# Forgetting-attention scores: two 64-row products per pair of heads and a separate product for the key decay, with two sets of probability buffers

## Chip, cores and metric

The kernel runs on one core of one Trainium2 chip. The metric is device time in microseconds (us) of one execution. All inputs, among them 227.94 MB of transfers by the profile, are read from device memory within that time.

## What is computed

The reference is a model of two blocks, each of two layers, over 512 tokens of 1024 features, in float32. The change touches one part of the first block's layers, the forgetting attention of six heads of 64 features:

```python
def fox_attention(q, k, v, log_f):
    c = jnp.cumsum(log_f, axis=1)                 # 512 tokens x 6 heads
    ...
        logits = jnp.einsum('bqhd,bkhd->bhqk', qb, k).astype(jnp.float32) * scale
        logits = logits + jnp.transpose(cb, (0, 2, 1))[..., None] - c_k
        causal = kpos[None, :] <= qpos[:, None]
        logits = jnp.where(causal, logits, NEG)
        w = jax.nn.softmax(logits, axis=-1)
        return jnp.einsum('bhqk,bkhd->bqhd', w.astype(v.dtype), v)
```

So every score of query q and key k gets c[q] - c[k] added, where c is the running sum of the log forget gates. A number added to a whole row of scores (c[q]) drops out of the softmax.

## The kernel before

Features lie on the partitions and tokens along the free axis. Large products are made from float32 values split into a high and a low part of type fp32r: `pe_tile` (L399) issues three matmuls of 512 columns (L404, L405, L406) for each tile of 128 features. Weights come as units of 128x1024: a transfer, a copy on ACT (L413, `w_hi`), a subtraction on POOL (L500, `w_lo`), then 24 matmuls.

Each layer of the first block runs, in this order on PE (`a_tensor`, L1187): the projection, the index scores (L1253), the forgetting attention ("fox", L1267), stick-breaking attention (L847 to L880), sparse attention ("dsa", L1282), and dense stages. Between the steps of the attention stages PE works off shares of 24 further units, the gate projection (`gate_share`); these are the rows L404 to L406 that stand between the attention's own.

Fox takes 12 pairs of heads and query blocks per layer: three pairs of heads, each with four blocks of 128 queries, so that the scores of a pair are 128, 256, 384 and 512 keys wide in turn. `pairs_pe`, `pairs_act` and `pairs_dve` write out the order by hand, each on its engine:

- PE, step n: scores of pair n+1 (L592, one product per head, then the mask L595), a share of gate tiles, the turning of pair n's probabilities (L605), another share, the products of pair n-1 with the values (L619). Where `ready` names a semaphore for the scores of pair n+1 (n+1 = 4 and 8), they stand behind the turning instead.
- DVE: row maxima of pair n+1 (L685), reciprocal and scaling of its probabilities (L693, L700), then one round of the index top-k search (L1560, L1562) and what `fox_after` adds. After pair 0 that is also the index-score work L1652, L1654.
- ACT: gate tiles that are due (L1363, L413), the exponentials of pair n+1 (L657), the copy of pair n's turned probabilities (L666).

The products of head e read `work[e]` and `work[2+e]`, 128 rows each: rows 0 to 63 are queries or keys, staged there by ACT (`fox_stage`, L1428), rows 64 to 127 are written by DVE (L1624, L1630) and carry c and selecting ones. With these four tiles taken, the probabilities have one set of buffers (`depth=1`): ACT's exponentials of pair n+1 wait until PE has turned pair n, and its copy of pair n waits for the value products of pair n-1.

In the sparse attention, heads 0 and 1 of a pair stand in rows 0 to 63 and 64 to 127 of the projection's tiles and are read there (`tile_rows`), as products of 64 rows.

Of the kernel before, what the change touches and what calls it, by code (L numbers as in the profile page):

```python
# [24 lines left out]
P = 128  # L25
# [52 lines left out]
C_ID, C_ROT, C_TRI, C_CAUS, C_STRICT, C_ST01, C_CHUNK = (P * n for n in range(7))  # L78
C_QA = 7 * P
C_QB = C_QA + 6  # L80
C_KA = C_QB + 6
C_KB = C_KA + 1
C_N = C_KB + 1

# [34 lines left out]
def plan(nc, ctx):  # L119
# [5 lines left out]
    def at(name, shape, dt, kb):  # L125
# [43 lines left out]
               for e, places in enumerate(((WK + 11.5, WK + 13.5, WK + 15, WK + 16), (128, WK + 16.5, 174, 175)))]  # L169
    S.c = at("log_f_sum", [P, SEQ], F32, WK + 16)  # L170
    o = [(WK + 18) * 1024]

# [73 lines left out]
    S.mask_ready = sem("mask_ready")  # L246
    S.fox_staged = sem("fox_staged")
    S.fox_aug = sem("fox_aug")
    S.stk_z = sem("stk_z")
# [304 lines left out]
class Pair:  # L554

    def __init__(self, S, n, b, key, mask, value, bank, heads=(0, 1), gate=None, first=None, begins=True, ends=True, depth=2):
        self.b, self.w = b, (b + 1) * P
        self.key = key
        self.mask = mask
        self.value = value  # L560
        self.bank = bank
        self.heads = heads
        self.gate = gate
        self.first = first
        self.begins, self.ends = begins, ends
        x = n % depth
        self.probs, self.turned = ((S.wk[4:6], S.wk[6:8]), (S.wk[0:2], S.wk[2:4]))[x]
        self.par = n % 2
# [11 lines left out]
def pairs_pe(S, pe, Z, h0, p0, pairs, ident, fill, ready, depth=2, lead=None):  # L580
# [3 lines left out]
    def scores(n):  # L584

        h = pairs[n]
        pe.wait_ge(Z.p, h0 + count_before(pairs, n))
        for sem, count in ready(n, "scores"):
            pe.wait_ge(sem, count)
        for e in h.heads:  # L590
            q, k = h.key(e)
            nc.tensor.matmul(S.X[e][:, 0:h.w], q, k, start=True, stop=False, skip_group_check=True)  # L592
        m, c = h.mask
        for e in h.heads:
            nc.tensor.matmul(S.X[e][:, c:h.w], S.idb[:, :], m, start=False, stop=True, skip_group_check=True).then_inc(Z.s, 1)  # L595
# [115 lines left out]
def fox_pairs(S):  # L711

    pairs = []
    for n in range(3 * QB):
        i, b = divmod(n, QB)
        w = (b + 1) * P
        pairs.append(Pair(S, n, b, lambda e, b=b, w=w: (S.wk[e][:, b * P:w], S.wk[2 + e][:, 0:w]), (S.causb[:, :], b * P),
                          lambda e, k, i=i: vt_head(S, k, V_FOX, 2 * i + e), (S.ps[3], S.X[3])[i % 2], depth=1))
    return pairs
# [467 lines left out]
def a_tensor(S, pe):  # L1187
    nc = S.nc
    ident = S.con[:, C_ID:C_ID + P]
    for L in range(DEPTH):  # L1190
# [68 lines left out]
        def fox_ready(n, what):  # L1259
            i = n // QB  # L1260
            if what == "scores" and n % QB == 0:
                return [(S.fox_staged, (L * 3 + i + 1) * 4), (S.fox_aug, (L * 3 + i + 1) * 2)]
            if what == "values" and n == 2 * QB:
# [92 lines left out]
def a_scalar(S, act, T):  # L1356
# [12 lines left out]
    for L in range(DEPTH):  # L1369
# [54 lines left out]

        def fox_stage(e, i):
            src = S.qkv[64 * e:64 * e + 64, :]
            for t, u in ((e, A_FQ), (2 + e, A_FK)):
                nc.scalar.activation(S.wk[t][0:64, :], cols2(src, u * SEQ, i, SEQ, SEQ), ACT.Copy).then_inc(S.fox_staged, 1)  # L1428

        act.wait_ge(S.rope_done, (L + 1) * len(ROPE))  # L1430
        for n, (b, h) in enumerate(idx_steps()):
            if n in (12, 16):
                fox_stage(n // 4 - 3, 0)
            act.wait_ge(S.idx_ready, L * 24 + n + 1)
# [14 lines left out]

        def fox_after(n):  # L1450
            if n % QB == 2 and n < 2 * QB:
                for e in range(2):
                    fox_stage(e, n // QB + 1)

        pairs_act(S, act, S.fox, L * 24, L * 12, fox_pairs(S), fox_after, depth=1,
                  before=lambda n: round_gates(FOX_FILL, n))
# [137 lines left out]
def a_vector(S, dve):  # L1594
    nc = S.nc
    for L in range(DEPTH):
# [24 lines left out]
        dve.drain()  # L1621
        nc.vector.tensor_copy(f, na)
        for e in range(2):
            nc.vector.tensor_scalar(S.wk[2 + e][64:128, :], na, S.con[64:128, C_KA:C_KA + 1], S.con[64:128, C_KB:C_KB + 1],  # L1624
                                    ALU.mult, ALU.add)

        def fox_rows(e, i):

            qa, qb = cols2(S.con[64:128, :], C_QA + e, i, 2, 1), cols2(S.con[64:128, :], C_QB + e, i, 2, 1)
            nc.vector.tensor_scalar(S.wk[e][64:128, :], f, qa, qb, ALU.mult, ALU.add).then_inc(S.fox_aug, 1)  # L1630

        dve.drain()
        for e in range(2):
            fox_rows(e, 0)

# [3 lines left out]
        for n, (b, h) in enumerate(idx_steps()):  # L1639
# [6 lines left out]
            else:  # L1646
                nc.vector.scalar_tensor_tensor(out=acc, in0=S.r[n % 2][:, 0:w], scalar=iw, in1=acc, op0=ALU.mult,
                                               op1=ALU.add).then_inc(S.idx_acc, 1)
            dve.drain()
        def index_scores():  # L1650
            for b in range(1, QB):
# [10 lines left out]
        def fox_after(n):  # L1662
            if n % QB == 2 and n < 2 * QB:
                for e in range(2):
                    fox_rows(e, n // QB + 1)
            if n == 0:
# [1050 lines left out]
def constants():  # L2717
# [11 lines left out]
    for h in range(6):  # L2729
        c[96 + h, C_QA + h] = 1.0  # L2730
        c[64 + h, C_QB + h] = 1.0
    c[64:96, C_KA] = -1.0
    c[96:, C_KB] = 1.0
    return c
# [40 lines left out]
```

## Time and profile before

| | |
|---|---|
| median of 3 executions | 2654.56 us (2651.69 to 2655.14) |
| the profiled execution | span 2653.1 us; no time of its own beside the span is given |
| PE busy | 2565.0 us, 97% |
| DVE, ACT, POOL busy | 59%, 43%, 40% |
| granted TensorE clock, mean over the span | 0.99 |

PE is TensorE's matmuls, DVE VectorE, ACT ScalarE, POOL GpSimd. A product of two float32 operands shows in the trace as two matmuls, so a pair of heads has four rows under L592. A matmul's length counts from its start to its end, and the next starts before that end; what a matmul costs is therefore read from one start to the next.

### The profile page before, as it was taken

How to read it: one execution, taken by the hardware profiler on the slowest of the kernel's cores; microseconds unless marked ns; L12 is line 12 of the kernel's file. 1: busy time of each engine (PE TensorE's matmuls, PEld its weight loads, DVE VectorE, ACT ScalarE, POOL GpSimd, SP SyncE). 2: the span in 40 equal slices, each digit the busy share in tenths (PEclk: the TensorE clock that was granted, in tenths of full speed). 3: DMA queues.
4: the chain of work that ended last, by engine and by line, in shares of the span. 5: the costliest groups of instructions: out<-in, count | busy, mean ns of one | idle time of the engine just before them, and what ended most of it. 6: DMA issues, size and time to landing. Idle time of an engine off the chain costs nothing.

```text
span 2653.1 us, 35398 instructions
## 1 busy us (share of the span) xinstructions
PE 2565.0 (97%) x12424; PEld 1983.9 (75%) x12424; DVE 1565.4 (59%) x2510; ACT 1147.6 (43%) x1984; POOL 1062.1 (40%) x440
## 2 busy tenths in 40 slices
PE   8999999999999899999999999998999999999998
PEld 6867667788888688676677888885887776887776
DVE  6147748843322751676588234227689766689765
ACT  3345444433322433544535233325247554347554
POOL 4432213354444344222233454442447512447512
PEclk9999999999999999999999999998999999999999
DMA  5321112233233243111122223231334211234211
GB/s 201 100 80 56 48 48 87 72 103 97 93 96 102 71 124 100 64 61 49 48 96 88 95 95 98 93 109 49 95 96 147 80 33 53 91 101 148 75 38 56
DMA packets 66891, 227.94 MB, mean 86 GB/s; under 512 B 8784, under 2 KB 8912, under 8 KB 66768
## 3 DMA queue, kind: packets, MB, share of 16 engines
q1 hardware_dynamic: 66192, 224.73, 26.2%
q8 instruction: 76, 1.25, 0.2%
q10 hardware_dynamic: 576, 1.57, 0.2%
q14 instruction: 47, 0.39, 0.0%
HBM read 216.57 MB, written 2.10 MB: 82 GB/s over the span
## 4 chain that ended last, share of the span: by engine, by line
PE 74%; DVE 12%; DVEq 9%; ACT 2%; issue 2%; POOL 0%; ACTq 0%; DMA 0%; SPq 0%
PE bank L404 20%; PE bank L406 19%; PE bank L405 19%; DVEq L2337 5%; PE bank L592 3%; PE bank L619 3%; PE bank L605 2%; PE bank L595 1%; PE bank L873 1%; DVEq L2359 1%; PE bank L1253 1%; PE bank L847 1%; DVE ffn_sum L1796 1%; PE bank L1225 1%; PE bank L1224 1%
## 5 line engine op out<-in xcount | busy, mean ns | idle before, releaser
L500 POOL TENSOR_TENSOR w_lo<-w_raw,w_hi 128x1024 fp32r<-128x1024 f32 x404 | 1017.8, 2527 | 1575.6 <-ACT w_hi L413 1569.7
L404 PE MATMUL bank<-x_hi,w_hi 128*128 128x512 f32 x2048 | 828.8, 405 | 28.3 <-DVE x_lo L2567 10.6
L406 PE MATMUL bank<-x_hi,w_lo 128*128 128x512 f32 x2048 | 804.9, 393 | 0.0
L405 PE MATMUL bank<-x_lo,w_hi 128*128 128x512 f32 x2048 | 803.5, 392 | 0.0
L413 ACT ACTIVATE w_hi<-w_raw 128x1024 fp32r<-128x1024 f32 x400 | 419.5, 1055 | 439.7 <-PE bank L406 355.3
L404 PEld LDWEIGHTS bank<-x_hi,w_hi 128*128 128x128 f32 x2048 | 388.4, 190 | 128.4 <-issue 29.7
L406 PEld LDWEIGHTS bank<-x_hi,w_lo 128*128 128x128 f32 x2048 | 387.8, 189 | 83.6
L405 PEld LDWEIGHTS bank<-x_lo,w_hi 128*128 128x128 f32 x2048 | 388.6, 190 | 75.0 <-issue 1.2
L404 PE MATMUL bank<-rhs_hi,w_hi 128*128 128x512 f32 x624 | 245.2, 393 | 3.3 <-DVE rhs_lo L1698 3.3
L405 PE MATMUL bank<-rhs_lo,w_hi 128*128 128x512 f32 x624 | 243.7, 390 | 0.0
L406 PE MATMUL bank<-rhs_hi,w_lo 128*128 128x512 f32 x624 | 243.4, 390 | 0.0
L1780 DVE TENSOR_TENSOR ffn_sum<-ffn_sum,bank 128x512 f32 x64 | 43.9, 688 | 286.3 <-PE bank L406 286.3
L657 ACT ACTIVATE work<-bank,neg_max 128x128 f32<-128x128 f32 (+3 forms) x216 | 112.0, 523 | 182.4 <-DVE neg_max L685 146.0
L1770 DVE TENSOR_TENSOR work<-work 128x512 f32<-128x512 f32 x64 | 93.9, 1467 | 135.1 <-ACT rhs_hi L1518 135.1
L2334 DVE SCALAR_TENSOR_TENSOR bank<-glu_out,params_b_cur,bank 128x512 f32<-128x512 f32 x216 | 152.7, 753 | 34.8 <-issue 34.8
L404 PEld LDWEIGHTS bank<-rhs_hi,w_hi 128*128 128x128 f32 x624 | 117.6, 188 | 33.5 <-issue 8.6
L406 PEld LDWEIGHTS bank<-rhs_hi,w_lo 128*128 128x128 f32 x624 | 117.6, 188 | 24.4
L405 PEld LDWEIGHTS bank<-rhs_lo,w_hi 128*128 128x128 f32 x624 | 117.5, 188 | 23.8
L685 DVE TENSOR_REDUCE neg_max<-bank 128x1 f32<-128x128 f32 (+3 forms) x216 | 96.1, 485 | 56.8 <-PE bank L595 55.1
L1516 ACT ACTIVATE work<-bank 128x512 f32<-128x512 f32 x64 | 37.9, 592 | 191.8 <-PE bank L406 183.9
L666 ACT ACTIVATE work<-bank 128x128 f32<-128x128 f32 (+3 forms) x216 | 83.1, 436 | 50.5 <-PE bank L619 31.6
L1772 DVE TENSOR_TENSOR rhs_lo<-work,rhs_hi 128x512 f32 x64 | 86.6, 1354 | 12.1 <-issue 12.1
(410 smaller groups left out, 3248.0 us busy)
## 6 DMA issues: line engine op xcount, KB each, us to landing
w_raw<-w SPq DMA_DIRECT2D x404, 512.0 KB, 3.4
work<-proj SPq DMA_DIRECT2D x60, 64.0 KB, 2.0
ln_in<-x SPq DMA_DIRECT2D x4, 512.0 KB, 7.2
out<-residual SPq DMA_DIRECT2D x8, 256.0 KB, 2.1
p_raw<-p ACTq DMA_DIRECT2D x2, 512.0 KB, 3.5
silu_z_nsa<-b_q SPq DMA_DIRECT2D x16, 64.0 KB, 2.3
work<-b_q SPq DMA_DIRECT2D x16, 64.0 KB, 2.3
silu_z_nsa<-b_kc SPq DMA_DIRECT2D x8, 64.0 KB, 2.0
```

The costliest lines, as they stand in the source:

```text
L404: nc.tensor.matmul(out, wh, xh, start=first, stop=False)
L405: nc.tensor.matmul(out, wh, xl, start=False, stop=False)
L406: S.last = nc.tensor.matmul(out, wl, xh, start=False, stop=last)
L413: S.nc.scalar.activation(S.wh[s][:, :], S.raw[s][:, :], ACT.Copy).then_inc(S.hi_ready[s], 1)
L500: S.nc.gpsimd.tensor_tensor(S.wl[s][:, :], S.raw[s][:, :], S.wh[s][:, :].bitcast(F32), ALU.subtract).then_inc(S.lo_ready[s], 1)
L657: nc.scalar.activation(h.probs[e][:, 0:h.w], S.X[e][:, 0:h.w], ACT.Exp, bias=S.nm[x][:, :], accum_out=S.rs2[:, x:x + 1]).then_inc(Z.p, 1)
L666: nc.scalar.activation(h.turned[e][:, 0:h.w], (S.X[2], S.ps[2])[e][:, 0:h.w], ACT.Copy).then_inc(Z.ptc, 1)
L685: nc.vector.tensor_reduce(S.nm[2 * h.par + e][:, :], S.X[e][:, 0:h.w], AX, ALU.max, negate=True).then_inc(Z.max, 1)
L1770: nc.vector.tensor_tensor(h, S.wk[j % 2][:, :], S.wk[j % 2][:, :], ALU.mult)
L1772: nc.vector.tensor_tensor(cols(S.rl, i * SLOTS + j), h, cols(S.rh, i * SLOTS + j).bitcast(F32), ALU.subtract).then_inc(S.ffn_h, 1)
L2334: stt(out=S.X[t % 2][:, :], in0=S.uc[:, bass.ds(i * 3 + (k + t * UC_W), SEQ)], scalar=S.curB[:, bass.ds(i * 3 + (k + PB_DW + t * CONV_K), ...
L2337: dve.drain()
```

## The change

The scores' product takes 64 rows per head straight from the projection's tiles. The key decay becomes a product of its own (`decay`): `cpick`, 64 rows by 128 columns of minus one in the two rows of the head, times `cparts`, in which row h holds the high part of c of head h and row 32+h the rest, both repeated in rows 64 to 127, in fp32r. The query's c is left out, as it drops out of the softmax. The staging copies on ACT and the augmented rows on DVE go; DVE fills `cparts` once a layer before the index scores and `cpick` right after them, where its place in memory comes free. Fox's pairs use two sets of probability buffers (`depth` 2).

```diff
--- before.py
+++ after.py
@@ -76,11 +76,8 @@
 
 
 C_ID, C_ROT, C_TRI, C_CAUS, C_STRICT, C_ST01, C_CHUNK = (P * n for n in range(7))
-C_QA = 7 * P
-C_QB = C_QA + 6
-C_KA = C_QB + 6
-C_KB = C_KA + 1
-C_N = C_KB + 1
+C_PART = 7 * P
+C_N = C_PART + 3
 
 
 PA_G1, PA_B1, PA_G2, PA_B2, PA_BF, PA_N = 0, 8, 16, 24, 32, 33
@@ -168,6 +165,8 @@
     S.stk_w = [[at(f"stick_weights{e}_{i}", [P, SEQ - i * P], F32, kb) for i, kb in enumerate(places)]
                for e, places in enumerate(((WK + 11.5, WK + 13.5, WK + 15, WK + 16), (128, WK + 16.5, 174, 175)))]
     S.c = at("log_f_sum", [P, SEQ], F32, WK + 16)
+    S.cparts = at("log_f_parts", [P, SEQ], F32R, WK + 16)
+    S.cpick = at("log_f_pick", [P, 3 * P], F32R, 128)
     o = [(WK + 18) * 1024]
 
     def small(name, n, dt=F32):
@@ -244,8 +243,7 @@
     S.relu_done = sem("relu_done")
     S.idx_acc = sem("idx_acc")
     S.mask_ready = sem("mask_ready")
-    S.fox_staged = sem("fox_staged")
-    S.fox_aug = sem("fox_aug")
+    S.fox_decay = sem("fox_decay")
     S.stk_z = sem("stk_z")
     S.stk_na = sem("stk_na")
     S.stk_ln = sem("stk_ln")
@@ -553,9 +551,10 @@
 
 class Pair:
 
-    def __init__(self, S, n, b, key, mask, value, bank, heads=(0, 1), gate=None, first=None, begins=True, ends=True, depth=2):
+    def __init__(self, S, n, b, key, mask, value, bank, heads=(0, 1), gate=None, first=None, begins=True, ends=True, depth=2, decay=None):
         self.b, self.w = b, (b + 1) * P
         self.key = key
+        self.decay = decay
         self.mask = mask
         self.value = value
         self.bank = bank
@@ -590,6 +589,9 @@
         for e in h.heads:
             q, k = h.key(e)
             nc.tensor.matmul(S.X[e][:, 0:h.w], q, k, start=True, stop=False, skip_group_check=True)
+        for e in h.heads if h.decay else ():
+            pick, parts = h.decay(e)
+            nc.tensor.matmul(S.X[e][:, 0:h.w], pick, parts, start=False, stop=False, skip_group_check=True)
         m, c = h.mask
         for e in h.heads:
             nc.tensor.matmul(S.X[e][:, c:h.w], S.idb[:, :], m, start=False, stop=True, skip_group_check=True).then_inc(Z.s, 1)
@@ -714,8 +716,9 @@
     for n in range(3 * QB):
         i, b = divmod(n, QB)
         w = (b + 1) * P
-        pairs.append(Pair(S, n, b, lambda e, b=b, w=w: (S.wk[e][:, b * P:w], S.wk[2 + e][:, 0:w]), (S.causb[:, :], b * P),
-                          lambda e, k, i=i: vt_head(S, k, V_FOX, 2 * i + e), (S.ps[3], S.X[3])[i % 2], depth=1))
+        pairs.append(Pair(S, n + 1, b, lambda e, b=b, w=w, i=i: (tile_rows(S, A_FQ + i, e)[:, b * P:w], tile_rows(S, A_FK + i, e)[:, 0:w]),
+                          (S.causb[:, :], b * P), lambda e, k, i=i: vt_head(S, k, V_FOX, 2 * i + e), (S.ps[3], S.X[3])[i % 2],
+                          decay=lambda e, w=w, i=i: (S.cpick[half(e), i * P:(i + 1) * P], S.cparts[half(e), 0:w])))
     return pairs
 
 
@@ -1257,9 +1260,8 @@
 
         pe.wait_ge(S.relu_done, (L + 1) * 24)
         def fox_ready(n, what):
-            i = n // QB
-            if what == "scores" and n % QB == 0:
-                return [(S.fox_staged, (L * 3 + i + 1) * 4), (S.fox_aug, (L * 3 + i + 1) * 2)]
+            if what == "scores" and n == 0:
+                return [(S.fox_decay, (L + 1) * 2)]
             if what == "values" and n == 2 * QB:
                 return [(S.fox.out, L * 3 + 1)]
             return []
@@ -1422,15 +1424,8 @@
                 if end == c:
                     gate_take(fill[0] + j)
 
-        def fox_stage(e, i):
-            src = S.qkv[64 * e:64 * e + 64, :]
-            for t, u in ((e, A_FQ), (2 + e, A_FK)):
-                nc.scalar.activation(S.wk[t][0:64, :], cols2(src, u * SEQ, i, SEQ, SEQ), ACT.Copy).then_inc(S.fox_staged, 1)
-
         act.wait_ge(S.rope_done, (L + 1) * len(ROPE))
         for n, (b, h) in enumerate(idx_steps()):
-            if n in (12, 16):
-                fox_stage(n // 4 - 3, 0)
             act.wait_ge(S.idx_ready, L * 24 + n + 1)
             if n >= 2:
                 act.wait_ge(S.idx_acc, L * 24 + n - 1)
@@ -1447,12 +1442,7 @@
             for x in range(2):
                 gate_takes(fill[i], calls[i], 2 * m + x)
 
-        def fox_after(n):
-            if n % QB == 2 and n < 2 * QB:
-                for e in range(2):
-                    fox_stage(e, n // QB + 1)
-
-        pairs_act(S, act, S.fox, L * 24, L * 12, fox_pairs(S), fox_after, depth=1,
+        pairs_act(S, act, S.fox, L * 24, L * 12, fox_pairs(S), lambda n: None,
                   before=lambda n: round_gates(FOX_FILL, n))
         round_gates(FOX_FILL, 3 * QB)
         nc.scalar.preload_act_table_set("natural_log_exp_and_others")
@@ -1619,19 +1609,12 @@
         dve.drain()
         nc.vector.tensor_tensor_scan(na, S.wk[4][64:128, :], f, 0.0, ALU.mult, ALU.add)
         dve.drain()
-        nc.vector.tensor_copy(f, na)
-        for e in range(2):
-            nc.vector.tensor_scalar(S.wk[2 + e][64:128, :], na, S.con[64:128, C_KA:C_KA + 1], S.con[64:128, C_KB:C_KB + 1],
-                                    ALU.mult, ALU.add)
-
-        def fox_rows(e, i):
-
-            qa, qb = cols2(S.con[64:128, :], C_QA + e, i, 2, 1), cols2(S.con[64:128, :], C_QB + e, i, 2, 1)
-            nc.vector.tensor_scalar(S.wk[e][64:128, :], f, qa, qb, ALU.mult, ALU.add).then_inc(S.fox_aug, 1)
-
+        nc.vector.tensor_copy(S.cparts[64:128, :], na)
         dve.drain()
-        for e in range(2):
-            fox_rows(e, 0)
+        rest = S.cparts[96:128, :]
+        nc.vector.tensor_tensor(rest, S.wk[5][96:128, :], rest.bitcast(F32), ALU.subtract)
+        dve.drain()
+        nc.vector.tensor_copy(S.cparts[0:64, :], S.cparts[64:128, :].bitcast(F32)).then_inc(S.fox_decay, 1)
 
         dve.wait_ge(S.bank_free[A_SPARE % SLOTS], G(A_SPARE) + 1)
         free_bank(S, dve, A_SPARE)
@@ -1647,6 +1630,10 @@
                 nc.vector.scalar_tensor_tensor(out=acc, in0=S.r[n % 2][:, 0:w], scalar=iw, in1=acc, op0=ALU.mult,
                                                op1=ALU.add).then_inc(S.idx_acc, 1)
             dve.drain()
+        for i in range(3):
+            m = nc.vector.tensor_copy(S.cpick[:, i * P:(i + 1) * P], S.con[:, C_PART + i:C_PART + i + 1].to_broadcast([P, P]))
+        m.then_inc(S.fox_decay, 1)
+
         def index_scores():
             for b in range(1, QB):
                 nc.vector.memset(S.sacc[0:64, SC0[b] + b * P + 64:SC0[b] + (b + 1) * P], NEG)
@@ -1660,9 +1647,6 @@
             nc.vector.tensor_copy(otok(S, tile)[rows, :], bank[rows, :]).then_inc(Z.out, 1)
 
         def fox_after(n):
-            if n % QB == 2 and n < 2 * QB:
-                for e in range(2):
-                    fox_rows(e, n // QB + 1)
             if n == 0:
                 index_scores()
             for x in range(2):
@@ -2727,10 +2711,8 @@
     c[:, C_ST01:C_ST01 + P] = i < j
     c[:, C_CHUNK:C_CHUNK + P] = np.where(j // 64 > i // 64, NEG, 0.0)
     for h in range(6):
-        c[96 + h, C_QA + h] = 1.0
-        c[64 + h, C_QB + h] = 1.0
-    c[64:96, C_KA] = -1.0
-    c[96:, C_KB] = 1.0
+        for part in range(2):
+            c[64 * (h % 2) + 32 * part + h, C_PART + h // 2] = -1.0
     return c
 
 
```

The order of the programs shows three places. First PE at the start of fox in the first layer, before the change; `work_96/97` are the keys, `work_94/95` the queries, `x_hi,w_hi` rows are gate tiles:

```order
L404 MATMUL bank<-x_hi,w_hi_54 128x512
L405 MATMUL bank<-x_lo,w_hi_54 128x512
L406 MATMUL bank<-x_hi,w_lo_58 128x512
L592 MATMUL bank<-work_96,work_94 128x128
L592 MATMUL bank<-work_97,work_95 128x128
L595 MATMUL bank<-causal_bf,ident_bf 128x128 x2
L404 MATMUL bank<-x_hi,w_hi_55 128x512
L405 MATMUL bank<-x_lo,w_hi_55 128x512
L406 MATMUL bank<-x_hi,w_lo_59 128x512
```

The same place after the change (the line numbers are those of the changed kernel):

```order
L402 MATMUL bank<-x_hi,w_hi_54 128x512
L403 MATMUL bank<-x_lo,w_hi_54 128x512
L404 MATMUL bank<-x_hi,w_lo_58 128x512
L591 MATMUL bank<-proj 128x128 x2
L594 MATMUL bank<-log_f_parts,log_f_pick 128x128 x2
L597 MATMUL bank<-causal_bf,ident_bf 128x128 x2
L402 MATMUL bank<-x_hi,w_hi_55 128x512
L403 MATMUL bank<-x_lo,w_hi_55 128x512
L404 MATMUL bank<-x_hi,w_lo_59 128x512
```

The two 128-row products became two 64-row products of `proj`, followed by the two decay products; the mask and the gate tiles behind it stand as before.

Second, PE around the first scores of the second pair of heads. Before the change, step 3 with its turning (x4 for each head) and the scores of pair 4 behind it:

```order
L406 MATMUL bank<-x_hi,w_lo_57 128x512
L605 MATMUL bank<-constants,work_98 128x128 x4
L605 MATMUL bank<-constants,work_99 128x128 x4
L592 MATMUL bank<-work_96,work_94 128x128
L592 MATMUL bank<-work_97,work_95 128x128
L595 MATMUL bank<-causal_bf,ident_bf 128x128 x2
L404 MATMUL bank<-x_hi,w_hi_53 128x512
```

After it, the scores of pair 4 behind the value products of pair 1 and ahead of the gate tiles:

```order
L621 MATMUL bank<-work_100,v_tok 64x128
L621 MATMUL bank<-work_101,v_tok 64x128
L591 MATMUL bank<-proj 128x128 x2
L594 MATMUL bank<-log_f_parts,log_f_pick 128x128 x2
L597 MATMUL bank<-causal_bf,ident_bf 128x128 x2
L402 MATMUL bank<-x_hi,w_hi_53 128x512
L403 MATMUL bank<-x_lo,w_hi_53 128x512
```

They moved forward past one share of gate tiles and the turning, to the place that they have in every other step.

Third, DVE at the end of the index scores, before:

```order
L1647 SCALAR_TENSOR_TENSOR idx_sum<-idx_relu_72,v_tok,idx_sum 128x512
L1647 SCALAR_TENSOR_TENSOR idx_sum<-idx_relu_73,v_tok,idx_sum 128x512
L685 TENSOR_REDUCE neg_max_115<-bank 128x1
L685 TENSOR_REDUCE neg_max_116<-bank 128x1
L693 RECIPROCAL gate_inv<-row_sums 128x2
```

and after the change, with the pick tiles between the last index sum and the first row maximum:

```order
L1630 SCALAR_TENSOR_TENSOR idx_sum<-idx_relu_72,v_tok,idx_sum 128x512
L1630 SCALAR_TENSOR_TENSOR idx_sum<-idx_relu_73,v_tok,idx_sum 128x512
L1634 CAST log_f_pick<-constants 128x128 x3
L687 TENSOR_REDUCE neg_max_119<-bank 128x1
L687 TENSOR_REDUCE neg_max_120<-bank 128x1
L695 RECIPROCAL gate_inv<-row_sums 128x2
```

PE's first scores wait for that last `log_f_pick` row (`fox_decay`), where they waited for ACT's and DVE's staging, long done, before.

## Rows read from the trace of the kernel before

**Rows 1.** The page, busy time of each engine over the span.
```profile
PE 2565.0 (97%) x12424; PEld 1983.9 (75%) x12424; DVE 1565.4 (59%) x2510; ACT 1147.6 (43%) x1984; POOL 1062.1 (40%) x440
```

**Rows 2.** Windows, fox, first layer: length, busy PE, PEld, DVE, ACT, POOL, clock, DMA.
```profile
187.00:270.50 83.50, 81.63 (x453) 60.45 (x452) 65.56 (x179) 38.97 (x96) 21.55 (x9) 1.00 0.16 51
```

**Rows 3.** Timeline of PE in fox: start, length, engine, line, what.
```profile
211.22 1.03 PE L605 MATMUL bank<-constants,work 128*128 128x128 f32 x8
212.36 0.68 PE L592 MATMUL bank<-work,work 128*128 128x128 f32 x4
212.88 0.28 PE L595 MATMUL bank<-causal_bf,ident_bf 128*128 128x128 bf16 x2
...
229.25 1.98 PE L592 MATMUL bank<-work,work 128*128 128x512 f32 x4
231.07 0.28 PE L595 MATMUL bank<-causal_bf,ident_bf 128*128 128x128 bf16 x2
...
266.65 1.04 PE L605 MATMUL bank<-constants,work 128*128 128x128 f32 x8
267.44 0.47 PE L404 MATMUL bank<-x_hi,w_hi 128*128 128x512 f32 x1
```

**Rows 4.** Timeline of PE in sparse attention, first layer, scores and masks.
```profile
366.05 0.49 PE L592 MATMUL bank<-proj 64*128 64x128 f32 x4
366.47 0.29 PE L595 MATMUL bank<-chunk_bf,ident_bf 128*128 128x128 bf16 x2
...
378.27 1.13 PE L592 MATMUL bank<-proj 64*128 64x512 f32 x4
379.33 0.60 PE L595 MATMUL bank<-sparse_mask,ident_bf 128*128 128x512 bf16 x2
```

**Rows 5.** Timeline of PE: from gate tiles into 64-row and 128-row products.
```profile
183.50 0.40 PE L406 MATMUL bank<-x_hi,w_lo 128*128 128x512 f32 x1
183.82 1.13 PE L1253 MATMUL bank<-proj 64*128 64x512 f32 x4
...
186.83 0.39 PE L406 MATMUL bank<-x_hi,w_lo 128*128 128x512 f32 x1
187.05 0.60 PE L592 MATMUL bank<-work,work 128*128 128x128 f32 x4
```

**Rows 6.** Timeline of PE in the second block: fp32r matmuls of 64 columns.
```profile
2057.96 0.28 PE L2057 MATMUL bank<-w_lo,cmp_hid_v_hi 128*128 128x64 f32 x1
2058.07 0.28 PE L2057 MATMUL bank<-w_hi,cmp_hid_v_lo 128*128 128x64 f32 x1
```

**Rows 7.** Timeline of PE: its waits in fox, idle time and releaser in brackets.
```profile
194.41 1.56 PE L592 MATMUL bank<-work,work 128*128 128x384 f32 x4 [1.17 <-ACT work L657]
...
201.55 1.98 PE L592 MATMUL bank<-work,work 128*128 128x512 f32 x4 [0.46 <-ACT work L657]
...
271.82 1.09 PE L619 MATMUL bank<-work,v_tok 128*64 128x128 f32 x16 [0.82 <-ACT work L666]
...
1110.51 1.98 PE L592 MATMUL bank<-work,work 128*128 128x512 f32 x4 [0.82 <-ACT work L657]
```

**Rows 8.** Timeline of DVE and POOL around the start of fox.
```profile
181.69 5.88 DVE L1647 SCALAR_TENSOR_TENSOR idx_sum<-idx_relu,v_tok,idx_sum 128x512 f32<-128x512 f32 x5 [1.30 <-ACT idx_relu L1438]
...
188.87 2.38 POOL L500 TENSOR_TENSOR w_lo<-w_raw,w_hi 128x1024 fp32r<-128x1024 f32 x1 [5.23 <-ACT w_hi L413]
...
189.77 1.76 DVE L700 TENSOR_SCALAR work<-work,gate_inv 128x128 f32<-128x128 f32 x2
```

**Rows 9.** Timeline of DVE at the program's start: casts of 128x128.
```profile
22.92 0.22 DVE L2570 CAST causal_bf<-constants 128x128 bf16<-128x128 f32 x1
23.05 0.22 DVE L2570 CAST strict_bf<-constants 128x128 bf16<-128x128 f32 x1
```

**Rows 10.** Timeline of DVE: start of step 0's index work, next row maxima.
```profile
195.20 0.26 DVE L1652 MEMSET idx_sum<- 64x64 f32 x3
...
199.67 1.02 DVE L685 TENSOR_REDUCE neg_max<-bank 128x1 f32<-128x384 f32 x2
```

## Prediction, on record before the result

> **What bounds the kernel now.** I read the page first: PE is busy 97% of the span, no other engine above 59% [rows 1], so only time taken from PE's own queue, or from its waits, can shorten the kernel. Then the windows of the changed stage: in fox of the first layer PE is busy 81.63 of 83.50 us, DVE 65.56, ACT 38.97 [rows 2]. The reader is to see two things there. PE's idle time is at most 1.87 us a layer, so the change can win little by removing waits; and DVE needs 65.56 / 12 = 5.5 us for a pair where PE takes 83.5 / 12 = 7.0, so DVE has slack on average but could be the bound in single steps. Last the timeline of PE, start to start, for what each product costs, and its bracketed waits.
>
> **The score products.** In fox the four matmuls of a pair (two heads, two passes each) cost 212.88 - 212.36 = 0.52 us at 128 keys and 231.07 - 229.25 = 1.82 at 512 [rows 3]. The sparse attention already reads its heads from rows 0 to 63 and 64 to 127, as fox will: 366.47 - 366.05 = 0.42 and 379.33 - 378.27 = 1.06 [rows 4]. The columns are the same, so the two heads there must run side by side for much of the time. The saving is 0.10 at 128 keys and 0.76 at 512. I take the line between them, 0.32 at 256 and 0.54 at 384: 1.72 for the four pairs of one pair of heads. Going from gate tiles into 64-row products costs 183.82 - 183.50 = 0.32 where 128-row ones cost 187.05 - 186.83 = 0.22 [rows 5]. That 0.10 falls on pairs 0 and 1 alone, which follow gate tiles; the others follow value products or turns. What lies on the way out, before the mask, is inside the differences above.
>
> The Trainium skill, "TensorEngine Tiling (Array Packing)", section Key Properties, says that changing the tiling mode drains TensorE, which speaks against this change: each pair now has a switch in front of and behind its products. By that rule, with two switches a pair at 0.1 each, 24 pairs would pay 4.8 us and the gain would be about 4 if nothing of it were in the rows yet. By the rows it costs 0.1 on the way in, and 0.42 against 0.52 stands with the way out in it. The sum goes by the rows.
>
> **The decay products.** Two more fp32r matmuls a pair, 64 rows each, one per head. fp32r gate matmuls of 512 columns follow one another at 0.22 [rows 5]. In proportion 384 columns cost 0.17 and 256 cost 0.12. A narrow one is dearer: 64 columns take 2058.07 - 2057.96 = 0.11 [rows 6], so by columns 128 take 0.22. If the two heads' products overlap as the scores do, a group of four pairs costs 0.22 + 0.12 + 0.17 + 0.22 = 0.73; if they don't, 1.46. I take 0.73, because the operands lie in the same two row halves and the outputs in the same two banks as the score products that do overlap. The lower end is nothing, if they ran under the other head's second score pass.
>
> **What else moves on PE.** The scores of pairs 4 and 8 no longer stand behind a turn. Eight turns cost 1.14 before such scores (212.36 - 211.22), 0.79 before gate tiles (267.44 - 266.65) [rows 3]; 0.35 goes twice a layer. With two sets of buffers ACT's copy for the last pair no longer waits for the value products before it, so PE's wait of 0.82 at 271.82 [rows 7] goes: its turn is over by about 267.5, and two copies end long before 271. The same stands in the second layer.
>
> **The start of fox.** Here the change adds a wait. PE began its first scores at 187.05 [rows 5]. Now they wait for the three pick tiles, which DVE writes behind its last index sum, ending at 181.69 + 5.88 = 187.57 [rows 8]. Casts of 128x128 follow at 23.05 - 22.92 = 0.13 and last 0.22 [rows 9]: 0.13 + 0.13 + 0.22 is about 0.5, and with 0.1 for the drain ahead the scores start at 188.2, 1.15 late. Behind them in PE's queue stands the whole stage. The bounds are 0.52 (casts free) and, if POOL's split gets in their way, 1.15 + 2.4 (below).
>
> **The first waits.** PE's waits of 1.17 at pair 2 and 0.46 at pair 3 [rows 7] came from ACT's exponentials being held until the turn. The first one goes. The second mostly does not, as DVE is late there: between scaling pair 1 and the row maxima of pair 2 it does index work from 195.20 to 199.67 [rows 10], 4.47, and PE's scores of pair 3 follow 1.88 behind those maxima (201.55 - 199.67). Before, the index work started 195.20 - 187.05 = 8.15 behind the first scores. After: the scores of pair 1 start about 3.0 behind them (nine gate matmuls at 0.22 to 0.24, the first scores, decay and mask), 1.05 later their mask ends, and maxima and exponentials take 1.7 (1.88 at 384 keys, above); with 0.85 for reciprocal and scaling (1.76 for two scalings beside POOL's split [rows 8], about half without) that is 6.6, an estimate. It is 1.55 sooner, less the start's 1.15: the scores of pair 3 start 0.4 earlier than before in the first layer, whatever PE saves until then. In the second, where the wait was 0.82 [rows 7] instead of 0.46, up to 0.8 earlier.
>
> **The sum.** From the scores of pair 3 on PE sets the pace. Pair 3: 0.76 - 0.22 = 0.54. Two groups: 2 x (1.72 - 0.73) = 1.98. Pairs 4 and 8: 0.70. Last wait: 0.82. That is 4.04, with 0.4 in front 4.4 in the first layer, and 4.6 (0.2 of the further 0.4 taken) in the second: 9.0 us.
>
> Worth nothing: ACT loses 24 staging copies, but it is busy under half of fox [rows 2] and PE waits there for DVE's chain, not for ACT's load. DVE loses its row tiles inside fox; that is slack for it, and it keeps DVE under PE's new pace: PE's step falls from 7.0 to about 6.6, DVE's from 5.5 to 5.3. In the projection DVE does three operations in place of five, of the same kind and width; they are covered by the wait for the index products, and uncovered they would still be no dearer. Weight units come at PE's pace, with POOL busy 21.55 of 83.50 [rows 2], so a faster PE does not run into them.
>
> Against the profiled span of 2653.1 this gives 2644.1; that span is 1.5 below the median, 2654.56, inside the scatter of the three runs. Against the median: **2645.6 us**.
>
> **Rivals.**
> 1. *The decay products don't overlap, or cost more than their columns.* Serial, they add 0.22 + 2 x 0.73 = 1.7 a layer behind pair 3: gain 5.6, 2649.0. For it: no row shows fp32r in 64-row tiles. Against: float32 ones overlap.
> 2. *The pick tiles collide with POOL.* POOL's split from 188.87 lasts 2.38, and DVE's two scalings of 128 columns beside it took 1.76 [rows 8], against 0.22 for a cast alone. Should the casts (187.6 to 188.2) meet it, the start slips by up to 2.4 a layer, and all of it reaches pair 3: gain 4.2, 2650.4. Against: 0.7 us lie between. The Trainium skill, "GPSIMD Engine Reference", says that the two engines share SBUF interfaces and that certain DVE instructions contend; by that rule too the delay comes only with an overlap in time.
> 3. *It is cheaper.* Decays under the score passes give back 0.22 + 2 x 0.73 = 1.7 a layer: gain 12.4, 2642.2.
> 4. *No change.* PE's gain is handed back in stick-breaking, where DVE or ACT would be late by as much: 2654. Against: that stage's start is set off by PE's own first product, and DVE finishes fox sooner, relative to it, than before.
> 5. *Slower.* One mechanism, at the decay products: in 64-row tiles they take, at every width, the pace of narrow ones, 0.11 per 64 columns, and one after the other. A group costs 2 x (0.22 + 0.44 + 0.66 + 0.88) = 4.4 instead of 0.73; six groups add 22, and less 9.0 the kernel is 13 slower: 2667. It decides from 2.2 us a group on. For it: 64 columns do go at that pace [rows 6]. Against: 512 columns don't [rows 5].
>
> **How the numbers follow.** Forecast 0.62 (gain 7 to 11), rival 1 0.11, rival 2 0.07, rival 3 0.10, rival 4 0.06, rival 5 0.04. The range goes from rival 3 to a little past rival 2, 2642.0 to 2651.0, and leaves out rivals 4 and 5 and some of the edges. This kernel's measurement can tell about 0.2%, 5.3 us, from no change. Faster by more: the forecast, rival 3, and a bit over half of rival 1, 0.79. Within: the rest of rival 1, rival 2, rival 4, 0.16. Slower: rival 5 and mishaps, 0.05.
>
> **What would show it.** In the changed profile: score pairs of 512 keys about 1.3 from their start to the mask; the first scores of fox about 1.1 later behind the last gate tile, with DVE's pick tiles as releaser; no wait for exponentials at pair 2, a small one at pair 3, none at the last value products; fox shorter by 4 to 5 us a layer, all other stages as long as before. I would be wrong if decay products stand one behind the other, if a wait for DVE appears in every step of fox, or if stick-breaking grows.

## The result, and the profile after

| | before | after |
|---|---|---|
| median | 2654.85 us (2651.69 to 2657.83, 4 runs) | 2641.14 us (2639.91 to 2646.33, 4 runs) |
| profiled span | 2653.1 us | 2640.5 us |
| mean granted TensorE clock of that execution | 0.990 | 0.993 |

The ratio is 0.995, 95% interval 0.9938 to 0.9962. The kernel became faster by half a per cent, as forecast, but by 13.7 us where 9.0 stood in the sum, and 2641.14 lies 0.9 us under the low end of the range. Two later sets of runs gave 0.9944 (0.993 to 0.9958) and 0.996 (0.9948 to 0.9972), with medians of 2641.08, again under the range, and 2644.04, inside it.

First the page after, busy time by engine. PE has 12 us less than in [rows 1], and bounds the kernel as before:

```profile
PE 2553.2 (97%) x12466; PEld 1976.1 (75%) x12472; DVE 1555.9 (59%) x2504; ACT 1134.6 (43%) x1960; POOL 1061.8 (40%) x440
```

The windows view of a stretch of fox after, first layer, columns as in [rows 2]. PE is busy all but 1.0 of 88.1 us:

```profile
184.90:273.00 88.10, 87.11 (x531) 64.10 (x527) 68.74 (x193) 41.23 (x100) 23.92 (x10) 1.00 0.21 66
```

The timeline of PE after, in fox of the first layer (start, length, engine, line, what, and in brackets a wait). These rows answer to [rows 3, 5, 7]:

```profile
187.36 0.39 PE L404 MATMUL bank<-x_hi,w_lo 128*128 128x512 f32 x1
188.70 0.46 PE L591 MATMUL bank<-proj 64*128 64x128 f32 x3 [0.94 <-DVE log_f_pick L1634]
...
194.83 0.92 PE L591 MATMUL bank<-proj 64*128 64x384 f32 x4
...
201.20 1.13 PE L591 MATMUL bank<-proj 64*128 64x512 f32 x4
201.76 0.79 PE L594 MATMUL bank<-log_f_parts,log_f_pick 64*128 64x512 f32 x2
202.49 0.29 PE L597 MATMUL bank<-causal_bf,ident_bf 128*128 128x128 bf16 x2
...
208.17 0.49 PE L591 MATMUL bank<-proj 64*128 64x128 f32 x4
208.41 0.31 PE L594 MATMUL bank<-log_f_parts,log_f_pick 64*128 64x128 f32 x2
208.65 0.28 PE L597 MATMUL bank<-causal_bf,ident_bf 128*128 128x128 bf16 x2
...
214.74 0.70 PE L591 MATMUL bank<-proj 64*128 64x256 f32 x4
215.49 0.28 PE L597 MATMUL bank<-causal_bf,ident_bf 128*128 128x128 bf16 x2
...
221.15 0.92 PE L591 MATMUL bank<-proj 64*128 64x384 f32 x4
222.17 0.29 PE L597 MATMUL bank<-causal_bf,ident_bf 128*128 128x128 bf16 x2
...
266.62 0.49 PE L850 MATMUL bank<-proj 64*128 64x128 f32 x4
267.04 1.09 PE L621 MATMUL bank<-work,v_tok 128*64 128x128 f32 x16
```

A pair of 512 keys with its decay takes 202.49 - 201.20 = 1.29, where the old product took 1.82; one of 128 keys 0.48 where it took 0.52. The wait at pair 2 (194.83) and the one at the last value products (267.04) are gone. One wait is new, for the pick tiles, at the first scores. In the second layer a wait of 0.4 for exponentials is left at pair 3. The two widths that the prediction took from a line stood at 0.96 and 1.40 in the kernel before, in the same view:

```profile
216.02 1.13 PE L592 MATMUL bank<-work,work 128*128 128x256 f32 x4
216.98 0.28 PE L595 MATMUL bank<-causal_bf,ident_bf 128*128 128x128 bf16 x2
...
222.63 1.56 PE L592 MATMUL bank<-work,work 128*128 128x384 f32 x4
224.03 0.28 PE L595 MATMUL bank<-causal_bf,ident_bf 128*128 128x128 bf16 x2
```

The timeline of DVE after, around the start of fox; it answers to [rows 8, 10]:

```profile
188.05 0.50 DVE L1634 CAST log_f_pick<-constants 128x128 fp32r<-128x128 f32 x3
...
194.84 0.26 DVE L1639 MEMSET idx_sum<- 64x64 f32 x3
...
199.32 1.02 DVE L687 TENSOR_REDUCE neg_max<-bank 128x1 f32<-128x384 f32 x2
```

**Where the time went.** I count fox from the last index-score product (the last L1253 row) to the first triangular product of stick-breaking (the first L873 row of the layer). That is the same work in every kernel here.

| profile | layer 1 | layer 2 | both | against before |
|---|---|---|---|---|
| before, both profiles | 93.42 | 93.82, 93.81 | 187.24 | |
| after, three profiles | 88.10, 88.07, 88.09 | 88.47, 88.52, 88.49 | 176.6 | -10.7 |
| one set of buffers (e3) | 91.05 | 91.66 | 182.71 | -4.5 |
| early pick tiles (e4, e11) | 87.55, 87.55 | 87.94, 87.93 | 175.5 | -11.8 |
| no decay (e5) | 86.56 | 86.93 | 173.5 | -13.8 |
| decay twice (e6) | 89.89 | 90.19 | 180.1 | -7.2 |
| two sets, old products (e7) | 90.39 | 90.78 | 181.2 | -6.1 |
| early pick, later round (e8, e12) | 86.93, 86.93 | 86.97, 86.97 | 173.9 | -13.3 |

The stage repeats to 0.05 us. So the change is worth 10.7 us in fox, and the rest of the 13.7 lies outside the stage that it touches. Stick-breaking, where rival 4 saw the gain handed back, takes 69.1 us from its first triangular product to its last, before and after.

### The profile page after: what moved, and what is told of

It reads as the page before. It is cut to its first block, busy times and chain, and to the rows that moved or that the text cites. A ratio compares the mean times of both kernels' runs of the same rounds, so it can differ in the third digit from the quotient of the medians.

```text
span 2640.5 us, 35446 instructions
## 1 busy us (share of the span) xinstructions
PE 2553.2 (97%) x12466; PEld 1976.1 (75%) x12472; DVE 1555.9 (59%) x2504; ACT 1134.6 (43%) x1960; POOL 1061.8 (40%) x440
## 4 chain that ended last, share of the span: by engine, by line
PE 72%; DVE 12%; DVEq 9%; ACT 3%; issue 2%; POOL 0%; DMA 0%; ACTq 0%; SPq 0%
PE bank L402 20%; PE bank L404 19%; PE bank L403 19%; DVEq L2321 5%; PE bank L621 3%; PE bank L591 3%; PE bank L607 2%; PE bank L597 1%; PE bank L876 1%; DVEq L2343 1%; PE bank L850 1%; DVE ffn_sum L1780 1%; PE bank L1256 1%; PE bank L1227 1%; PE bank L1228 1%
```

## The experiments

**The clock outside fox (e1, e2, e9).** No edit: both kernels once more, to draw more runs and profiles.

> The kernel before, unchanged, once more. Theory A (the change is worth what it takes out of fox, 10.7 us in the traces, and the rest of the 13.7 us between the medians is half-rate stretches of the TensorE clock that fall elsewhere from run to run): median between 2651 and 2657, and the half-rate stretches of this profile stand partly at other places than in the first one. Theory B (the change also gains about 3 us outside fox, each time): the stretches stand where they stood.

> The changed kernel, unchanged, once more. Theory A: fox again 5.3 us a layer shorter, and the ratio to the kernel before moves toward 0.996 (2644 us) as more runs are drawn; the stretches outside fox stand elsewhere than in its first profile. Theory B: again 13 to 14 us faster, 2641, with the same few stretches at the same places.

> The changed kernel, unchanged, a third time, for the clock: fox is 10.7 us shorter in every profile, the medians say 13.7 and 14. Theory A (the rest is a higher mean granted clock that its runs happened to draw): here its mean clock is nearer to the 0.991 of the runs of before, and the gain nearer to 11. Theory B (the changed kernel has the higher clock each time, because its stages stand elsewhere in time): 0.993 again, gain 13 to 15.

Measured: before against itself 0.9999 (0.9989 to 1.0009), 2655.56 us, with runs from 2650.19 to 2660.33. After: 2641.08 in its second set of runs, 2644.04 in its third. The view of the cores gives the mean granted clock of a profiled execution. Before again, after again and after a third time:

```profile
core 0: 2655.3 us, clock 0.992
```

```profile
core 0: 2639.8 us, clock 0.993
```

```profile
core 0: 2642.2 us, clock 0.992
```

Each run here comes with its span and this mean clock (of the first four runs of before, only the profiled one does, and they are left out); it is below 1 because in short stretches TensorE runs at 1.2 GHz and not at 2.4. A span goes with it:

| mean clock of the run | before: runs, mean span | after: runs, mean span | difference |
|---|---|---|---|
| 0.990 | 23, 2654.9 | 2, 2646.0 | 8.9 |
| 0.993 | 17, 2650.2 | 9, 2640.5 | 9.7 |
| all | 59, 2653.4 at 0.9912 | 15, 2640.9 at 0.9928 | 12.5 |

A fit of the span over all runs of all kernels, one level for each kernel and one slope for the clock, gives 1.5 us for 0.001 of mean clock with a residual of 1.3 us, and puts after 10.1 us below before. Fox says 10.7. So 10 to 11 us are the change, and the rest goes with the clock: 2.4 of the 12.5 between the means, about 3 of the 13.7 between the medians.

The profiles show the same by stages. Here are the lengths outside fox, fox counted as above, with the time at 1.2 GHz that lies in them, summed from the trace's record of the clock:

| profile | from the start to fox | between the fox stages (at 1.2 GHz) | behind the second (at 1.2 GHz) |
|---|---|---|---|
| before | 184.4 | 815.2 (6.8) | 1466.3 (44.9) |
| before again | 187.0 | 817.4 (10.2) | 1463.7 (34.7) |
| after | 184.9 | 817.1 (10.2) | 1462.0 (28.1) |
| after again | 184.6 | 817.0 (10.2) | 1461.6 (27.8) |
| after, third | 185.0 | 817.3 (10.2) | 1463.4 (32.6) |

With 6.8 us at half rate the middle takes 815.2, with 10.2 it takes 817.0 to 817.4, before and after alike. Behind the second stage, 0.27 us taken off for each us at half rate (an estimate from these rows) leaves 1454.1 to 1454.6 in all five. So the work outside fox costs what it did, and its length differs by the clock alone; the start differs from run to run.

A half-rate stretch can be seen in the windows view of before, second block, and is missing in that of the first profile of after, where the same work stands some 10 us earlier (the granted clock is the third number from the end). Before, then after:

```profile
2045.00:2065.00 20.00, 20.00 (x93) 16.70 (x92) 13.43 (x33) 15.99 (x22) 11.83 (x6) 0.92 0.31 106
2100.00:2120.00 20.00, 19.41 (x128) 12.69 (x127) 13.88 (x31) 13.11 (x36) 12.21 (x7) 0.93 0.18 54
```

```profile
2035.00:2055.00 20.00, 19.51 (x98) 16.60 (x99) 14.89 (x35) 17.54 (x24) 12.78 (x6) 1.00 0.35 121
2089.00:2109.00 20.00, 19.40 (x137) 12.77 (x138) 14.75 (x36) 14.13 (x38) 12.33 (x7) 1.00 0.21 59
```

Of theory A, what holds is that the gain outside fox is clock and nothing else: the third set of runs of after had one at 0.990 too, and its gain was 10.6 us by the ratio of 0.996. That the stretches fall at chance is not shown. Some do move: before has one at 1311 and before again has none there. Others stand with the kernel. Both profiles of before have a stretch at 2045 to 2047 and none from 1860 to 2040; all three of after have one at 1974 and none from 1980 to 2085. The profiles of the kernels below fall in the same two groups: e7, with the old products, has one at 2040, and the other seven one between 1971 and 1981. Before, before again, after and after a third time:

```profile
1860.00:2040.00 180.00, 176.49 (x811) 143.67 (x810) 149.18 (x175) 84.02 (x112) 100.81 (x41) 1.00 0.36 113
1860.00:2040.00 180.00, 176.48 (x812) 143.63 (x811) 148.55 (x184) 82.62 (x111) 98.61 (x40) 1.00 0.35 112
1974.00:1979.00 5.00, 5.00 (x17) 3.93 (x16) 4.68 (x8) 1.87 (x4) 0.84 (x1) 0.66 0.22 54
1974.00:1979.00 5.00, 4.09 (x11) 3.27 (x12) 4.74 (x9) 0.56 (x2) 2.15 (x1) 0.66 0.15 36
```

The mean clock of after was also the higher one in each set of runs that had both kernels, 0.9932 against 0.9912 and 0.9923 against 0.9915. Against theory B stands that the kernel with early pick tiles (e4, e11), which does the same work about 1 us earlier, had 0.9911 over ten runs, like before. So whether after's lead of some 2 us by the clock belongs to it or was drawn stays open. A kernel that was to shift fox by more, with the casts of the pick tiles written five times (e10), gave no time.

**One set of probability buffers (e3).** The changed kernel with

```diff
-    decay=lambda e, w=w, i=i: (...)))
+    depth=1, decay=lambda e, w=w, i=i: (...)))
...
-        pairs_act(S, act, S.fox, L * 24, L * 12, fox_pairs(S), lambda n: None,
+        pairs_act(S, act, S.fox, L * 24, L * 12, fox_pairs(S), lambda n: None, depth=1,
```

> The changed kernel with one set of probability buffers (depth 1) and all else kept. Theory A (two sets are worth the waits for exponentials and the last wait): fox about 2.3 us a layer longer than in the changed kernel, 4.6 in all, a wait of about 1 us at pair 2 and of 0.8 at the last value products are back. Rival (DVE's index work bounds the start of fox anyway, so only the last wait counts): 0.9 us a layer, 1.8 in all.

Measured: 2647.77 us, ratio 0.9971 (0.9959 to 0.9983); fox 182.7, 6.1 more than after. Theory A had named 4.6, the rival 1.8. Three waits are back in the timeline of PE, first layer, and the one at pair 3 is larger than in before:

```profile
195.94 0.92 PE L591 MATMUL bank<-proj 64*128 64x384 f32 x4 [1.17 <-ACT work L659]
...
203.10 1.13 PE L591 MATMUL bank<-proj 64*128 64x512 f32 x4 [0.83 <-ACT work L659]
...
269.83 1.09 PE L621 MATMUL bank<-work,v_tok 128*64 128x128 f32 x16 [0.82 <-ACT work L668]
```

The wait for the pick tiles stays. So the second set of buffers is more than half of what fox gained.

**Two sets with the old products (e7).** The kernel before, its staging tiles put in memory that is free during fox:

```diff
+    S.stage = [at(f"fox_rows{n}", [P, SEQ], F32, 170 + 2 * n) for n in range(4)]
...
-        pairs.append(Pair(S, n, b, lambda e, b=b, w=w: (S.wk[e][:, b * P:w], S.wk[2 + e][:, 0:w]), ...
-                          ..., (S.ps[3], S.X[3])[i % 2], depth=1))
+        pairs.append(Pair(S, n + 1, b, lambda e, b=b, w=w: (S.stage[e][:, b * P:w], S.stage[2 + e][:, 0:w]), ...
+                          ..., (S.ps[3], S.X[3])[i % 2]))
...
-        pairs_act(S, act, S.fox, L * 24, L * 12, fox_pairs(S), fox_after, depth=1,
+        pairs_act(S, act, S.fox, L * 24, L * 12, fox_pairs(S), fox_after,
```

> The kernel before with its four staging tiles at another place in memory and so with two sets of probability buffers; 128-row products, staging and order kept. Theory A (buffers and products add up): fox 187.2 less the 6.1 that the second set was worth in the changed kernel, 181.1. Rival (the second set pays only with the new products and their earlier scores, because the staged pairs hold PE up): 184 or more.

Measured: 2647.54 us, ratio 0.9976 (0.9967 to 0.9985); fox 181.2, as theory A said to 0.1. With e3 this is a square of four kernels: the second set is worth 6.1 with either kind of product, the new products with their decay 4.5 to 4.6 with either number of sets. That 4.6 holds all that came with the products: the earlier place of the scores of pairs 4 and 8 too, since e7 keeps their staging and order, and the wait at the start as a loss. PE's waits in fox of the first layer are down to one:

```profile
PE bank L593 <- ACT work L658: 0.5, 1, 0.5
```

**What the decay products cost (e5, e6).** They are left out, or issued twice:

```diff
-        for e in h.heads if h.decay else ():
+        for e in tuple(h.heads) * 2 if h.decay else ():
```

> The changed kernel without the decay products, so that the scores lack the forget term. Fox is counted from the last index-score product to the first triangular product of stick-breaking; it was 176.6 us for both layers in the changed kernel. Theory A (the decay products add what the start-to-start distances show, 0.06, 0.11, 0.18 and 0.23 at the four widths): 1.4 to 1.8 us less a layer, 2.8 to 3.5 in all. Rival (part of that distance is a drain that stays without them): under 2 in all.

> The changed kernel with each decay product issued twice, so that the forget term counts double. Theory A (the first pair hides a part under the score passes, a second one costs its columns): 0.6 to 0.75 us for a group of four pairs, 3.2 to 3.8 in all. Rival (the two heads' decay products don't overlap each other): twice that, over 6.

Measured: without, fox is 3.1 us shorter; twice, 3.5 longer. Both are where theory A had them. Without them PE waits 0.2 us longer in each layer at pair 3 (0.2 and 0.6 where after has none and 0.4), so the decays cost PE some 3.5 and not 3.1. The timeline of PE at the second pair of 512 keys, without and then twice:

```profile
227.31 1.13 PE L591 MATMUL bank<-proj 64*128 64x512 f32 x4
228.37 0.28 PE L594 MATMUL bank<-causal_bf,ident_bf 128*128 128x128 bf16 x2
```

```profile
228.44 1.03 PE L594 MATMUL bank<-log_f_parts,log_f_pick 64*128 64x512 f32 x4
229.41 0.29 PE L597 MATMUL bank<-causal_bf,ident_bf 128*128 128x128 bf16 x2
```

Issued twice, the decays at 512 keys take 229.41 - 228.44 = 0.97 from their start to the mask; issued once they take 202.49 - 201.76 = 0.73. So a second decay for both heads costs 0.24. One full-array matmul of 512 columns costs 0.22 [rows 5], so the two heads' decays run side by side. At 128 keys, issued twice:

```profile
208.21 0.49 PE L591 MATMUL bank<-proj 64*128 64x128 f32 x4
208.81 0.29 PE L597 MATMUL bank<-causal_bf,ident_bf 128*128 128x128 bf16 x2
```

That is 0.60 where after takes 0.48, so a second decay for both heads costs 0.12 here, and the first cost 0.06. At 256 keys the second costs 0.12 as well, 0.87 less the 215.49 - 214.74 = 0.75 of after: a narrow decay has a price of its own, and only the first one gets half of it for nothing.

**The start of fox (e4, e11).** The pick tiles get a place in memory that is free earlier, and are written right behind the parts:

```diff
-    S.cpick = at("log_f_pick", [P, 3 * P], F32R, 128)
+    S.cpick = at("log_f_pick", [P, 3 * P], F32R, 176)
```

> The changed kernel with the pick tiles at another place in memory, written right behind the parts, long before fox. Theory A (the start's wait of 0.94 plus the issue behind it is passed on in full): PE starts fox about 1.1 us sooner behind the last gate tile and each layer is 1.1 us shorter, 2.2 in all. Rival (DVE's index work bounds pair 3 whatever the start does): the start is sooner, a wait at pair 3 takes its place, no gain.

> The kernel with the early pick tiles once more: its fox is 1.1 us shorter than the changed kernel's, its median was 3.5 us longer at a mean clock of 0.9908 against 0.993. Theory A: now another mean clock, median 2636 to 2645. Theory B: again 0.991 and 2644.

Measured: fox 1.1 us shorter in both layers together, half of what theory A said. PE starts without a wait, and then, at the scores of pair 3, waits for the exponentials of pair 2, behind DVE's index work, as the rival said (0.5 in the first layer, 0.9 in the second); the rival's "no gain" went too far:

```profile
200.25 1.13 PE L591 MATMUL bank<-proj 64*128 64x512 f32 x4 [0.52 <-ACT work L659]
```

The medians are 2644.54, ratio 0.995 (0.9936 to 0.9964), and in the second set of runs 2642.6 at a mean clock of 0.9914, 0.9954 (0.9941 to 0.9967). Of its ten runs five had a mean clock of 0.990, and the one at 0.994 had a span of 2635.8, shorter than any of after. That second median lies where theory A of e11 had it, but its clock is so near to 0.991 that it doesn't decide between the two theories. By medians nobody would have seen that this kernel is the better one; by the stage it is, twice, and the fit puts it 2.4 us below after at equal clock.

**The first top-k round later (e8, e12).** On top of the early pick tiles:

```diff
-            for x in range(2):
+            for x in (0, 1) * (0 if n == 0 else 2 if n == 7 else 1):
                 top_round(S, dve, x)
```

> The kernel with the early pick tiles, and the first top-k round moved from behind pair 0 to behind pair 7. Theory A (the waits of 0.5 and 0.9 at pair 3 that took the place of the start's wait come from DVE's work behind pair 0): both go, fox 175.5 falls to 174.1. Rival (two rounds behind pair 7 make DVE late there): a wait of 1 us or more at pairs 9 or 10, no gain. For the clock: at the same mean granted clock its span is 12 us below that of before, whatever the medians say.

> The kernel with early pick tiles and the later top-k round once more, beside the changed kernel on one chip: fox 2.7 us shorter in both layers together. Its time at equal mean clock is 2 to 3 us below the changed kernel's; the medians follow the clock.

Measured: fox 173.9, both times, 2.7 under after; no wait of PE is left in fox, at pair 3 or behind pair 7, in either layer. The timeline of DVE shows why: the row maxima of pair 2 start 0.84 behind the copy that prepares the index scores, not 4.2:

```profile
194.77 0.26 DVE L1639 MEMSET idx_sum<- 64x64 f32 x3
195.10 0.76 DVE L1641 COPY idx_score<-idx_sum 128x1152 f32<-128x1152 f32 x1
195.94 1.02 DVE L687 TENSOR_REDUCE neg_max<-bank 128x1 f32<-128x384 f32 x2
```

Medians 2641.15 and 2641.98, ratios 0.9952 (0.9939 to 0.9966) and 0.9951 (0.9939 to 0.9964). At a mean clock of 0.993 its four runs have 2638.9 where after has 2640.5, and before 2650.2: 11.3 below before, where 12 was expected. The fit puts it 12.5 below before and 2.4 below after, the same as the kernel with early pick tiles alone. So it is the best of these kernels by the stage; at equal clock it can't be told from early pick tiles alone, and by medians it can't be told from after.

## Why the prediction was right and wrong

**Right.** PE's own queue sets the pace, and both reasons for the gain were the ones named. The score product at 512 keys takes 1.29 with its decay (1.28 by the sum); the start slips by 188.70 - 187.36 = 1.34 less the usual 0.22, so 1.12 (1.15 by the sum, in which two small errors cancel: the last index sum ended 0.15 sooner behind PE than thought, and PE started 188.70 - 188.55 = 0.15 behind the last cast, for which the sum had nothing); the 0.35 behind turns is gone twice a layer (scores of pair 4 follow value products, and 208.65 - 208.17 is their whole cost); the last wait is gone. Rivals 1, 2, 4 and 5 did not come: decays overlap (e6), the casts ended at 188.55 with no sign of POOL, stick-breaking takes as long as before, and from 256 columns on they go by their columns. The switch of tiling mode, on which the Trainium skill's "TensorEngine Tiling (Array Packing)", Key Properties, warns, cost no more than the 0.1 of [rows 5]: with early pick tiles (e4), where no wait hides it, the first scores follow the gate tile by 187.27 - 186.95 = 0.32, against 0.22 before, and what the products save is measured up to the mask, with the way out in it.

**Off in size, inside fox: 10.7 for 9.0.** By the sum's own terms, first layer:

| term | predicted | measured |
|---|---|---|
| up to the scores of pair 3 | 0.4 | (201.55 - 187.05) less (201.20 - 187.59), 0.89 |
| pair 3 | 0.54 | 1.82 - 1.29 = 0.53 |
| two groups of four | 1.98 | 2 x (4.70 - 3.54) = 2.32 |
| pairs 4 and 8 | 0.70 | 0.70 |
| last wait | 0.82 | (271.82 - 270.51) less (267.04 - 266.62), 0.89 |
| layer | 4.4 | 5.3 |

The second layer gained 93.82 - 88.47 = 5.35 where the sum had 4.6.

Here 187.59 is where the first scores would have started without their wait (187.36 and the usual 0.23). In the first term DVE's index work starts 194.84 - 188.70 = 6.1 behind the first scores, where my chain of estimates gave 6.6: the scores of pair 1 came 2.8 behind the first (I had 3.0), and from the row maxima to the reciprocal it took 1.5 (I had 1.7). In the third, a group costs 0.48 + 0.75 + 1.02 + 1.29 = 3.54: the decays add 0.06, 0.12, 0.17 and 0.23 to the 64-row products, 0.58, where I had 0.73. All of the difference is at 128 keys, where I took twice the 0.11 of 64 columns, 0.22, and the product adds 0.06. By e6 a pair of decays costs 0.12 there when it stands behind another one, so 128 columns are no dearer than 64, and about half of even that is hidden behind the scores. Rival 3 had the decays under the score passes at every width; it is true by half of the narrowest alone.

**What failed: the step from the sum to the time.** "Against the median" subtracts 9.0 from 2654.56, and the range has no term for the clock outside the changed stage. The three runs shown then spread over 3.5 us; 59 spread over 10, from 2650 to 2660, with mean clocks of 0.988 to 0.993, at 1.5 us per 0.001. The measured four runs of after had 0.990 to 0.995. About 10.7 of the 13.7 is fox. The remaining 3.0 goes with the clock: the table by stages shows no other difference outside fox, and the mean clock was 0.993 in these four runs against 0.9912 over 59 of before. With 10.7 in place of 9.0 the forecast would have been 2643.9, inside the range; the 1.7 missing in fox and the clock together put the median under it. That it came near the low end at all, where rival 3 stood, is no credit to rival 3, whose mechanism did not come at full size. What puts a half-rate stretch here or there, and whether the change itself does, is not settled.

**Where two sets of buffers and the products meet.** The sum treated them as parts of one ledger and named no split. e3 and e7 give it: 6.1 for the second set, 4.6 for the products. The first paragraph of the prediction was wrong on this: it read that PE was idle for at most 1.87 us a layer and that removing waits could win little. The window of [rows 2] ends at 270.50, ahead of the last wait, of 0.82, and the second set was worth 3.0 us a layer. The removal of 24 staging copies was rightly priced at nothing for ACT's load, but it is what makes the room for the second set: without that, staging had to move elsewhere, as in e7.

## What to carry to other kernels

Where PE is over 95% busy, price a change by start-to-start distances in the stage itself, and judge it there: the stage repeated to 0.05 us while the time of the whole kernel moved by 10. Compare whole times at equal mean clock, and give a forecast's range a term for the clock. When a queue is freed from one wait, look for what is next in line: the start's 1.1 us came back by half, until the work on DVE that stood behind it was moved too. A wait for a buffer (depth) can be worth more than the products that one set out to speed up.

## What the runs showed of the hardware

- Float32 and fp32r products of 64 rows, one per half of the rows and each to its own bank, run side by side: 1.06 us for two heads of 512 columns in two passes each, where 128-row products take 1.82, and 0.24 for two fp32r products (e6).
- Fp32r products of 128 columns behind such a pair add 0.06 for two heads, and a second such pair 0.12, as much as one of 256 columns (e6).
- Going from full-array gate tiles into 64-row products costs 0.32 us from start to start, against 0.22 into 128-row ones (before, and e4).
- The mean granted clock of one and the same program lay between 0.988 and 0.993 in 59 runs, and its span moved with it, by 1.5 us for each 0.001. Ten runs of the kernel with early pick tiles did not show its 2 us by medians.
